# Gated delta rule, second pass: two heads' steps side by side in one queue order

## The reference, cut to what matters

```
a   = I + strict_lower(kb @ k.T * decay)                 # per chunk
u,w = solve(a, [v * beta, kb * exp(gcum)])               # triangular solve
def step(S, chunk):
    v_new = u - w @ S
    o     = (q * exp(gcum)) @ S + (q @ k.T * decay) @ v_new
    S     = S * exp(g_last) + (k * exp(g_last - gcum)).T @ v_new
```

## Time and profile before

| | |
|---|---|
| median of three runs | 4195.68 us (4190.52 to 4205.33) |
| the profiled execution | 4194.11 us, of which the span is 4192.3 us |
| busy in the span | TensorE 92%, VectorE 61%, GpSimd 31%, ScalarE 29% |
| mean granted clock of TensorE | 0.967 of full speed |
| first pass | about 1467 to 1602 us of the span |
| second pass | about 1602 to 1894 us of the span |

### The profile page before, as it was taken

How to read it: one execution, slowest core, us unless ns; L and a number is a source line. 1 busy time by engine, 2 the same in 40 slices (tenths; PEclk the granted TensorE clock), 3 DMA queues, 4 the chain that set the end, 5 groups by cost and what they waited for, 6 DMA issues and landing times. The chain is left out here.

```text
span 4192.3 us, 53471 instructions
## 1 busy us (share of the span) xinstructions
PE 3870.7 (92%) x19878; PEld 2820.9 (67%) x19878; DVE 2551.6 (61%) x4594; ACT 1205.3 (29%) x2519; POOL 1304.3 (31%) x1515
## 2 busy tenths in 40 slices
PE   8899999999999797888999999989999989669998
PEld 4577555555555586777888886568755566668887
DVE  7634899652488884557688876645534428923354
ACT  3155310101222484652121112128611221341112
POOL 1175399200000068820000094849000111530001
PEclk9999999999999899999999999999999999879999
DMA  4542366331111076544345554523011375882222
GB/s 171 196 112 90 122 179 186 116 112 62 58 70 50 21 226 164 118 98 163 129 154 177 173 165 127 154 61 114 19 53 63 124 257 191 246 237 93 76 86 76
DMA packets 287968, 533.16 MB, mean 127 GB/s; under 512 B 177024, under 2 KB 184064, under 8 KB 263424
## 3 DMA queue, kind: packets, MB, share of 16 engines
q1 hardware_dynamic: 216736, 344.70, 25.5%
q0 software_dynamic: 53312, 180.00, 14.3%
q10 hardware_dynamic: 17696, 5.56, 0.6%
HBM read 430.01 MB, written 100.01 MB: 126 GB/s over the span
## 5 line engine op out<-in xcount | busy, mean ns | idle before, releaser
L570 PE MATMUL P<-hu,ring 128*128 128x384 f32 (+1 forms) x2448 | 743.0, 457 | 6.0 <-PEq L849 3.6
L570 PEld LDWEIGHTS P<-hu,ring 128*128 128x128 f32 x2448 | 465.5, 190 | 258.7 <-issue 5.8
L887 PE MATMUL P<-area,ring 128*128 128x256 f32 (+1 forms) x1880 | 484.4, 413 | 29.5 <-PEq L2605 16.0
L887 PEld LDWEIGHTS P<-area,ring 128*128 128x128 f32 x1880 | 356.1, 191 | 147.8 <-issue 38.4
L570 PE MATMUL P<-area,ring 128*128 128x256 f32 (+1 forms) x1584 | 443.2, 432 | 3.7 <-DVE area L733 3.0
L570 PEld LDWEIGHTS P<-area,ring 128*128 128x128 f32 x1584 | 301.7, 191 | 127.9 <-issue 5.4
L887 PE MATMUL P<-area,hu 128*128 128x256 f32 (+1 forms) x1104 | 297.2, 424 | 5.5 <-DVE hu L1010 5.5
L1147 POOL TENSOR_TENSOR fold<-mod,vec 128x16 f32<-128x16 f32 (+1 forms) x5 | 10.1, 2018 | 862.6 <-DMA s_fb<-area 365.0
L887 PEld LDWEIGHTS P<-area,hu 128*128 128x128 f32 x1104 | 209.3, 190 | 84.2 <-DVE hu L1010 7.7
L3010 DVE SCALAR_TENSOR_TENSOR area<-area 128x1024 f32<-128x1024 f32 x124 | 189.6, 1529 | 17.4 <-ACT area L3086 15.3
L2478 POOL TENSOR_TENSOR area<-area 128x512 f32<-128x512 f32 (+2 forms) x98 | 177.1, 1807 | 7.7
(11 more groups left out here) (495 smaller groups left out, 7193.4 us busy)
## 6 DMA issues: line engine op xcount, KB each, us to landing
ring<-in_w_ffn_in SPq DMA_DIRECT2D x44, 1024.0 KB, 4.8
area<-in_w_mod SPq DMA_DIRECT2D x70, 512.0 KB, 3.5
ring<-s_c POOLq DMA_DIRECT2D x18, 1152.0 KB, 9.4
stat<-in_w_mod SPq DMA_DIRECT2D x40, 512.0 KB, 3.4
s_c<-area POOLq DMA_DIRECT2D x32, 576.0 KB, 3.2
ring<-in_w_ffn_out SPq DMA_DIRECT2D x24, 704.0 KB, 4.1
area<-s_b POOLq DMA_DIRECT2D x16, 1024.0 KB, 6.0
hu<-s_c POOLq DMA_DIRECT2D x14, 1152.0 KB, 9.7
```

Of the source, the lines that this page charges most:

```text
L570: last = mm(to, col(a, k), b[:, k, :], start=fresh and k == 0, stop=k == q - 1, skip_group_check=True)
L887: last = mm(to, a[:, 128 * k:128 * k + 128], b[k], start=fresh and k == 0, stop=k == q - 1, skip_group_check=True)
```

## The change

The second pass goes through stages k = -2 to 31. A stage holds one of the steps 2 to 5 of a head (`main(k)`, s = k % 4 + 2) and, where s is 4 or 5, beside it the step 0 or 1 of the next head (`ahead(k)`). S, R, VW and VN get a second buffer, and `PA` and `PB` of a direction share one bank, so that two heads' parities have four banks; `grow` now waits for the `VN` copy too (`vc`), and the early `values` of step 0 for `kept_o`. `outward` writes into the banks of the done head's parity. The eight squares of a head stand in one stage. The work on a half head's inverse begins up to two half heads ahead in place of one, with a third `XT` buffer, which VectorE zeroes at the end of the first pass. SP issues `fin_load(2)` and `diag_load(2)` ahead of the stages, and later ones about a half head earlier against the steps than before, `diag_load` in front of `fin_load`; from half head 11 on GpSimd issues `diag_load` after its solve. The solve takes 128 blocks at a time, one a partition, in six sets in place of eight.

The diff, cut to what is spoken of:

```diff
-    XT = [half(cut(u, 1536 * n, 1536)) for n in range(2)]
     NTA = [cut(u, 3072, 2304), cut(tmp, 0, 2304)]
     NT = [half(x[:, 0:1536]) for x in NTA]
-    S, R, VW, VN = (cut(u, 3072 + 512 * n, 512).rearrange("p (d v n) -> p d v n", d=2, v=2) for n in range(4))
+    S, R, VW, VN = ([x.rearrange("p (d v n) -> p d v n", d=2, v=2) for x in (cut(u, 3072 + 512 * n, 512), cut(tmp, 1024 + 512 * n, 512))]
+                    for n in range(4))
     o_sum = [cut(tmp, 0, 1024).rearrange("p (t v n) -> p t v n", t=4, v=2), cut(stat, 0, 1024).rearrange("p (t v n) -> p t v n", t=4, v=2)]
...
     near, far = ([mats(cut(H, 2304 * n + o, 768), 128) for n in range(2)] for o in (0, 768))
     x_lead, x_tail = ([mats(cut(H, 2304 * n + o, 192), 32) for n in range(2)] for o in (1536, 1728))
...
+    prod = cut(ring, 3072, 256)
+    SETS = 6
+    sets_of = lambda hh: range(48 * hh // 128, (48 * hh + 47) // 128 + 1)
     dvn = lambda x: x.rearrange("p (d v n) -> p d v n", d=2, v=2)
     GT = [dvn(x) for x in (cut(ring, 3328, 512), cut(ring, 3840, 512), cut(tmp, 2304, 512), cut(ring, 5120, 512))]
...
-    PA, PB = ([bank(2 * k + d) for d in range(2)] for k in range(2))
+    PA, PB = ([[bank(2 * p + d, 256, o) for d in range(2)] for p in range(2)] for o in (0, 256))
...
+    ahead = lambda k: ((k + 2) // 4, (k + 2) % 4) if (k + 2) % 4 < 2 and k + 2 < 4 * HEADS else None
+    BY_POOL = 11
 
     def both_ways(x, s, twice):
...
                 i, h = hh // 2, hh % 2
-                sp.wait_ge(xw[i], 32)
+                for g in sets_of(hh):
+                    sp.wait_ge(xw[g], 32)
...
-                if hh >= 2:
-                    sp.wait_ge(vn, per6(*order[3 * (hh - 1) - 1], 1))
+                for g in sets_of(hh):
+                    sp.wait_ge(xw[g], 32)
+                done = (xt_first if hh < 3 else xt_in if hh < BY_POOL else xt_last)[hh % 3]
+                if hh == 2:
+                    sp.wait_ge(third, 1)
+                elif hh > 2:
+                    i, s = order[3 * (hh - 2) - 1]
+                    sp.wait_ge(vn[i % 2], per6(i, s, 1))
+                    i = hh // 2
                 for b in range(4):
                     of = slice(32 * b, 32 * b + 32)
                     for d, k in ((0, "xb"), (1, "xa")):
-                        sp.dma_start(six(XT[hh % 2][of, d])[:, :, 32 * b:32 * b + 32],
+                        sp.dma_start(six(XT[hh % 3][of, d])[:, :, 32 * b:32 * b + 32],
...
             load_kt(1)
-            for n, (i, s) in enumerate(order):
-                hh = n // 3
-                if s % 3 == 0 and 1 <= hh < 15:
-                    diag_load(sp, hh + 1)
-                if s >= 2 and 4 * i + s + 1 < 32:
-                    load_at(4 * i + s + 1)
-                if s % 3 == 1 and hh + 2 < 16:
-                    fin_load(sp, hh + 2)
-                if s == 5 and i + 2 < HEADS:
-                    load_kt(i + 2)
+            fin_load(sp, 2)
+            diag_load(sp, 2)
+            for k in STAGES:
+                q = k // 2
+                if 3 <= k + 3 < 4 * HEADS:
+                    load_at(k + 3)
+                if k % 2 and 3 <= q + 3 < BY_POOL:
+                    diag_load(sp, q + 3)
+                if k % 2 and 3 <= q + 4 < 16:
+                    fin_load(sp, q + 4)
+                if k % 4 == 3 and k // 4 + 2 < HEADS and k >= 0:
+                    load_kt(k // 4 + 2)
             sp.wait_ge(f6, 16)
+            sp.wait_ge(vn[1], per6(HEADS - 1, 2, 1))
             sp.dma_start(c.h[:, :, 0:LAT], c.spill[:, :, 0:LAT]).then_inc(h_back, 16)
...
             load(0)
-            for i in range(HEADS):
-                x = NB[i % 2]
...
+                x = NB[g % 2]
+                pool.wait_ge(nb_in[g], 16)
                 for j in range(1, 31):
                     n = 31 - j
                     y = prod[:, 0:n * j].rearrange("p (r c) -> p r c", r=n)
-                    step(P_.tensor_tensor(y, x[:, j + 1:32, j:j + 1].broadcast_to([96, n, j]),
-                                          x[:, j:j + 1, 0:j].broadcast_to([96, n, j]), ALU.mult))
+                    step(P_.tensor_tensor(y, x[:, j + 1:32, j:j + 1].broadcast_to([128, n, j]),
+                                          x[:, j:j + 1, 0:j].broadcast_to([128, n, j]), ALU.mult))
...
-                    if (i, j) == (1, 14):
+                    if j == 24 and g + 1 < SETS:
+                        load(g + 1)
...
+                    elif (g, j) == (1, 16):
                         diag_load(pool, 1)
                 step(P_.memset(x.rearrange("p r c -> p (r c)")[:, 0:1024:33], 1.0))
-                if i:
-                    pool.wait_ge(xw[i - 1], 32)
+                if g:
+                    pool.wait_ge(xw[g - 1], 32)
...
-                    pool.dma_start(c.gdn[k][i].rearrange("h d u b n -> (h d u b) n"), of.rearrange("p r c -> p (r c)")).then_inc(xw[i], 16)
...
+            pool.wait_ge(xw[SETS - 1], 32)
+            for hh in range(BY_POOL, 16):
+                diag_load(pool, hh)
 
         @block.tensor
...
             def outward(i, v):
 
                 pe.wait_ge(unit, i + 1)
-                pe.wait_ge(oq, 8 * min(i + 2, HEADS))
-                if i == HEADS - 1:
-                    pe.wait_ge(kept_o, 2 * i - 1 + v)
                 for t in range(4):
-                    last = nc.tensor.transpose(bank(4 + v, 128, 128 * t), o_sum[i % 2][:, t, v, :], c.ident[:, :])
+                    last = nc.tensor.transpose(bank(2 * (i % 2) + v, 128, 128 * t), o_sum[i % 2][:, t, v, :], c.ident[:, :])
                 last.then_inc(turn_o, 1)
             turns(0)
             grams(0)
...
+
+                p = i % 2
+                pe.wait_ge(vw[p], per5(i, s, d))
...
                 if s >= 2:
...
+                    pe.wait_ge(vc, per4(i, s - 2, d))
+                mm(PA[p][d], KT[p][:, chunk[d][s], :], VW[p][:, d].rearrange("p v n -> p (v n)"), start=True, stop=True).then_inc(sn[p], 1)
...
+            for k in STAGES:
+                q, now, soon = k // 2, main(k), ahead(k)
+                if now:
+                    asks(*now)
+                if soon and soon[1]:
+                    asks(*soon)
+                if k % 2 == 0 and 1 <= q + 1 < 16:
+                    whole(q + 1)
+                elif k % 2 and 1 <= q + 2 < 16:
+                    blocks64(q + 2)
+                if now:
+                    i, s = now
+                    values(i, s, 0)
+                    asked(k, i, s, 0)
+                    values(i, s, 1)
+                    if s < 5:
+                        grow(i, s, 0)
+                    asked(k, i, s, 1)
+                    if s < 5:
+                        grow(i, s, 1)
+                    if s == 4 and i:
+                        outward(i - 1, 0)
+                        outward(i - 1, 1)
+                if soon:
+                    values(*soon, 0)
+                    values(*soon, 1)
+                if k % 2 == 0 and 1 <= q + 2 < 16:
+                    blocks32(q + 2)
+                elif k % 2 and 1 <= q + 2 < 16:
+                    cross64(q + 2)
+                if now:
+                    attended(k, *now)
+                if soon:
+                    grow(*soon, 0)
+                    grow(*soon, 1)
+            for v in range(2):
+                outward(HEADS - 1, v)
...
-                copy(qkv[:, 16 + 2 * i + v, 0:LAT], bank(4 + v), scale=gain).then_inc(kept_o, 1)
+                copy(qkv[:, 16 + 2 * i + v, 0:LAT], bank(2 * (i % 2) + v), scale=gain).then_inc(kept_o, 1)
...
+            def weighted(i, s):
+
+                p = i % 2
                 for d in range(2):
-                    act.wait_ge(vn, per6(i, s, d))
+                    act.wait_ge(vn[p], per6(i, s, d))
                     if s < 5:
                         for v in range(2):
-                            last = copy(VW[:, d, v, :], PB[d][:, 128 * v:128 * v + 128], scale=col(i, 3, s, d, v))
-                        last.then_inc(vw, 1)
-                if s >= 2:
-                    for d in range(2):
-                        copy(VN[:, d], pair(PB[d][:, 0:256])).then_inc(vc, 1)
-                if hh + 1 < 16:
-                    (keep32, keep64, keep_whole)[k3](hh + 1)
-                if i >= 2 and s == 1:
-                    outward(i - 2, 0)
-                    outward(i - 2, 1)
-                if i:
-                    if s == 2:
-                        squares(i - 1, (0,))
-                    elif s == 3:
-                        squares(i - 1, (1, 2))
-                    elif s == 4:
-                        squares(i - 1, (3,))
-                    elif s == 5:
-                        act.wait_ge(mean, i)
-                        nc.scalar.activation(rs, rs, ACT.Sqrt).then_inc(root, 1)
-            i = HEADS
-            squares(i - 1, range(4))
-            for v in range(2):
-                outward(i - 2, v)
-            act.wait_ge(mean, i)
```

(134 more changed lines are left out.)

155 lines of the change are left out of this document (51 added, 104 removed).

## The result

The changed kernel took 4209.97 us in the median of six runs against 4193.36 for the kernel before: a ratio of 1.0030 (95% interval 1.0019 to 1.0040). Measured once more it was 4205.01 (12 runs) against 4196.36, ratio 1.0018 (1.0009 to 1.0027). So it is slower by one to four parts in a thousand; 4196 had been said, with a range of 4168 to 4214. The profiled execution took 4203.17 us, its span is 4201.4, 9.1 more than before.

A forecast was written before the change was run, and what follows sets the result against it. One dependent chain through TensorE, ScalarE and VectorE, with TensorE's order deciding, was taken to bound the kernel; -0.9 + 0.8 + 3.2 - 0.8 = +2.3 on the profiled 4194.1 gave 4196 us, range 4168 to 4214.

The forecast's parts named there:

- The sum: Whole kernel: start -0.9, six heads +0.8, last head +3.2, tail -0.8, together +2.3 us.
- the way to the `asks` of (1, 2): First pass and head 0 up to head 1's step 2: 1652.7 against 1653.60, so -0.9 us.
- the last head: From the `asks` of (7, 2) to head 7's first square: 24.9 against 21.7 us, +3.2.
- the tail: End of second pass: head 6's two outward copies no longer stand before the square root, -0.8 us.
- the three mechanisms: Squares in one place, `keep64` behind weighted copies, outward copies before early `values`: about 6 us a head given back.
- the likeliest case: Whole kernel about unchanged: 4196 us, own range 4184 to 4208, chance 0.57.
- the base of the sum: The profiled execution of the kernel before, 4194.11 us, to which 2.3 was added.
- GpSimd's shorter solve: Six sets instead of eight end some 79 us earlier, near 1750; hidden by the pass, so gain nothing.
- TensorE's pace: Rival, second pass: waits overlap and heads fall to TensorE's busy time, 32.3 us; about 4170, chance 0.22.
- The clock: Rival, stage of step 3: waits of 1.7 and 1.3 lower the clock, 3 us a head; 4214, chance 0.12.
- GpSimd's time with partitions: Rival, solve: a set of 128 partitions takes 52.3 us instead of 39.25, delaying loads; 4241, chance 0.03.
- Late transfers: Rival, second pass: SP falls behind again and the 15.7 us of transfer waits return; +12, 4208, chance 0.06.

The follow-up runs named there:

- the loads alone: The kernel before with a third `XT` and loads issued a half head earlier, steps, squares and solve unchanged; ratio 0.9977 to the kernel before.
- the last version: Changed kernel with squares in two places, `cross64` later, outward through the queries' banks, and in step 5 `keep64` before the `VN` copies; 4177.18 us, ratio 0.9955.
- The squares experiment: Changed kernel with a head's eight squares split, four in the stage of step 2 and four in that of step 3; ratio 1.0012 to the kernel before.
- the loads and the solve alone: The kernel before with third `XT`, earlier loads and the solve in six sets of 128, without the staging of two heads; ratio 0.9962.

## Why the prediction was right and wrong

**The sum was right for the pair of profiles.** Against the profile before, the way to the `asks` of (1, 2) is 1.4 shorter (0.9 said), six heads take 220.4 (1870.91 - 1650.52; 219.6 said), the last head 24.4 to the first square at 1895.29 (24.9 said), the tail is 0.7 shorter (0.8 said): +2.2, where +2.3 was said. The stages were said to be 7.3, 9.4, 10.6 and 9.3 and are 7.0, 9.3, 10.6 and 9.8. Each of the three mechanisms was at its place, and the edit that removes it gives its time back; all together, with the wait that one of them left, they gave 4.5 us a head where the prediction put about 6. That the sum met this pair to 0.1 is luck, as the next paragraph shows. So in part is that 4209.97 lies in the stated range: the likeliest case had ended at 4208, and what lay above was there for a fall of the clock that did not come. The second measurement, 4205.01, lies in that case's own range.

**What failed is the base of the sum**, the step that took the profiled execution as it was. Its heads (447.0) were 5.0 longer than in the second profile of the same kernel, 1.7 of them by one fall of the clock that the second does not have, so a pair of profiles can't carry a sum of 2 us. The mean of two makes it +4.9, the second profile alone +7.4. The timed ratios ask for 7.5 to 12.6, with their intervals for 3.8 to 16.8. Whether anything beyond the heads is slower is open: the stages outside them scatter by 15 us, which is enough to hold the difference, but no run shows a cause.

**A wrong step that the sum didn't show:** that GpSimd's shorter solve is worth nothing. No row of the kernel before had a wait for it, and alone it gained no time (1.0001), but the cover went with the early loads. With the loads alone SP waited 14.3 us for the solve; with the solve as well the heads were 10.3 shorter, of which 7.9 lie behind the first `values`. The ratios, 0.9977 and 0.9962, put it at 6 us with intervals that overlap. In the staged kernel itself the old solve was not tried. GpSimd's stores in the changed kernel:

```profile
1626.23 0.59 POOL L1973 DMA_DIRECT2D gdn_xa<-ring  x1 [0.30 <-POOL ring L1971]
...
1665.38 0.59 POOL L1973 DMA_DIRECT2D gdn_xa<-ring  x1 [0.30 <-POOL ring L1971]
...
1744.78 0.59 POOL L1973 DMA_DIRECT2D gdn_xa<-ring  x1 [0.30 <-POOL ring L1971]
```

A set takes 39.15 here, and the last one leaves at 1744.78, over 70 us before the loads alone had theirs: so no early load has to stand for it.

**The rivals.** TensorE's pace: not in this kernel, but 32.1 a head, just under the 32.3 that this rival gave, is what the last version reaches once the waits are gone. The clock: in the changed kernel it stayed at 1.00 from head 1 on, behind waits of 1.49 too. The squares experiment had one fall, behind two shorter waits close together, and in the second profile of the kernel before it stayed at 1.00 behind 3.16. So the length of one wait, between 1.6 and 2.15, does not decide it, as the prediction had it. The Trainium skill ("TensorE: Matmul & The Clock Gate", A second HAM failure mode) tells of frequent short idle times that make the clock swing; the changed kernel, with four waits of about a microsecond or more in each head, doesn't bear that out; the one stretch at 0.50 in the squares run fits it. GpSimd's time with partitions: 39.15 a set of 128, as good as the 39.25 with 96. Late transfers: none after half head 2. The zeroing of the third `XT`, taken as 1.7, took 1.34. TensorE waited 2.14 for the first state behind it, but then 1.5 and 3.2 more for the transfers of half head 2, which hid it.

## What to carry to other kernels

When two chains are laid side by side in engines that work in order, whatever stands in front of a chain's copy can hold the chain: here the eight squares cost it 1.1 us a head. Look on every engine for what can stand behind it, or in an idle gap in front: four such moves took 4.5 us off a head of 36.6. Split a change that has several parts: here one half gained 16 us and hid that the other lost 21; with its waits mended the staging has heads 8.5 us shorter than the loads and the solve alone, but the timed ratios (0.9955 and 0.9962) can't tell the two apart. And before a sum of two microseconds is believed, profile the kernel before twice.

## What the runs showed of the hardware that was not expected

In two profiles of one program the granted clock went two ways behind the same wait: 0.50 from 1622 to 1628 behind 3.18 us, 1.00 behind 3.16. The program's heads differed by 5.0 us between these profiles, with nearly equal waits for transfers, while the changed kernel's three profiles with the same order on TensorE (449.2, 449.6, 449.3) agree in 0.4. What lies outside the heads ranges over 15 us, whatever the kernel.
